# Products of zeros on TensorE between the steps of three mixture-of-experts routers

## The chip, the cores and the metric

The kernel runs on one core of a Trainium2 chip. The metric is the device time of one launch in microseconds (us), the median over several runs. TensorE's clock has two levels in what follows, 1.2 and 2.4 GHz, which the profile writes as a granted clock of 0.50 and 1.00.

## The reference

The reference runs one layer of a first block and two layers of a second block on 256 tokens of width 1024, all in float32. Each of the three layers ends in a hierarchical mixture of experts. Its router is what matters here:

```python
g_logits = jnp.dot(t, w_rg).astype(jnp.float32) + b_rg          # 4 groups
g_idx = jnp.argmax(g_logits, axis=-1)
e_logits = (jnp.dot(t, w_re) + b_re).reshape(n_tok, 4, 8)       # 32 experts
e_sel = e_logits[rows, g_idx]                                   # those of the chosen group
top_v, top_i = lax.top_k(e_sel, 2)
top_w = jax.nn.softmax(top_v, axis=-1) * g_w[:, None]
for g in range(N_GROUPS):
    h = silu(einsum('td,edf->tef', t, w_gate[g])) * einsum('td,edf->tef', t, w_up[g])
    out = out + einsum('tef,efd->td', h * combine[:, g, :, None], w_down[g])
```

Every token goes to two of 32 experts. The experts' hidden width is 256 in the first layer and 512 in the other two, so the expert weights are 100.7 MB and twice 201.3 MB, and they are most of what the kernel reads.

## The kernel before, in words

**Parts.** The program is a straight line for each engine, with semaphores between them. On TensorE it goes: mixers of layer 1, `moe("e1")`, mixers of layer 2, `moe("e2")`, mixers of layer 3, `moe("e3")`. The function `moe` of the TensorE block (lines 737 to 916) has a router, a loop over experts, and a branch for experts with too many tokens.

**Router, on TensorE.** `residual` (or, in e2 and e3, code in the main program) computes the last output projection (line 663, 1106 or 1150) and transposes the first 128 tokens (line 643). `moe` then

- multiplies the first 128 tokens by the router's weights (line 750, 8 matmuls of 36 columns);
- waits for VectorE to finish the second 128 tokens, first half (`_tok1a`) and second half (`_tok`), and transposes them in two groups of four (`turn_to_T`, line 643);
- waits until ScalarE (line 1197) and VectorE (line 1465) have copied those transposes out of PSUM, and multiplies them by the router's weights (line 750 again);
- writes zeros into PSUM banks 0 to 3 with one product each of the bfloat16 tile `no_sum`, which holds zeros (line 757); the scatter matmuls of the loop add to these banks later;
- waits for VectorE's choice of experts (`_sel`, lines 1646 to 1670) and counts the rank of each token within its expert by five small float32 matmuls (lines 761 to 765, "the rank matmuls") into bank 7;
- waits for VectorE to turn ranks into a selection matrix S (lines 1676 to 1697; `_split`), and gathers the tokens of the first step's experts by 32 matmuls (`gather`, line 774) into banks 4 and 7;
- waits until ScalarE and VectorE (line 1711) have copied those, and begins the loop with the first gate products (line 820).

**Loop over experts.** A step takes 4 experts in e1 and 2 in e2 and e3: gate and up products (line 820), the next step's gather (774), transposes (829, 834), down products (852), scatter (864). There are 8 steps in e1 and 16 in each of e2 and e3.

**Weights.** SyncE issues all loads of weights into `ring`, six slots of 2 MB, which hold the weights of exactly one step. The first step's weights are loaded before or during the router (lines 526 to 530); the load of a later step's weights into a slot waits until the matmuls that read the slot are done (lines 516 to 518, `used[hs]`). 

**PSUM banks.** A table made in Python (`plan`, `uses`) says which use of each bank is which; `bank_free[b]` counts the reads that free bank b, and TensorE waits for that count before it writes a bank again. Bank 7 is free from the last attention on until the rank matmuls; banks 0 to 3 hold zeros or sums of the scatter from line 757 on.

Of the kernel before, what the change touches and what calls it, by code (L numbers as in the profile page):

```python
# [28 lines left out]
P = 128  # L29
# [58 lines left out]
def build(nc, ins, out):  # L88
    ctx = ExitStack()
    with ctx:  # L90
        _build(ctx, nc, ins, out)


def _build(ctx, nc, ins, out):
    def sb(name, shape, dt=F32):
        return ctx.enter_context(nc.sbuf_tensor(name, shape, dt))
# [3 lines left out]
    def flag(name):  # L100

        if name not in sems:
            sems[name] = ctx.enter_context(nc.semaphore(name))
        return sems[name]
# [12 lines left out]
    no_sum = sb("no_sum", [P, 512], mybir.dt.bfloat16)  # L117
# [130 lines left out]
    psum = ctx.enter_context(nc.psum_tensor("psum", [P, 8, 512], F32))  # L248
# [4 lines left out]
    bank_free = [flag(f"bank_free{b}") for b in range(8)]  # L253
    plan, uses = {}, [0] * 8

    def use(name, bank):
        plan[name] = (bank, uses[bank])
        uses[bank] += 1
# [3 lines left out]
    def use2(*name):  # L262
        use(name, turn[0] % 2)
        turn[0] += 1
# [38 lines left out]
    for n in range(4):  # L303
        use2("res1", n)

    def plan_moe(name):
        for n in range(4):
            use((name + "xT", n), (4, 5, 2, 3)[n] if name == "e3" else 2 + n)
        use((name + "logits",), 6)
        use((name + "rank",), 7)  # L310

    plan_moe("e1")
    before_moe = {"e1": list(uses)}
    use(("memk",), 5)
# [11 lines left out]
    for n in range(4):  # L326
        use(("res2", n), 2 + n)
    plan_moe("e2")
    before_moe["e2"] = list(uses)
    plan_turn("x3T", 4)  # L330
# [11 lines left out]
    for n in range(4):  # L342
        use(("res3", n), (0, 1, 2, 3)[n])
    plan_moe("e3")
    before_moe["e3"] = list(uses)

    def open_bank(pe, *name):

        b, m = plan[name]
        if m:  # L350
            pe.wait_ge(bank_free[b], m)
        return b

    def close_bank(ins, *name):
        ins.then_inc(bank_full[plan[name][0]], 1)
# [10 lines left out]
    def evacuated(eng, *name):  # L366

        b, m = plan[name]
        eng.wait_ge(bank_free[b], m + 1)
# [19 lines left out]
    for part, (names, width) in enumerate(zip(STREAM, (3, NSLOT, NSLOT))):  # L389
# [5 lines left out]
        e = f"e{part + 1}"  # L395
# [7 lines left out]
    def load_chunk(sp, c):  # L403
        s, _, prior = where[c]
        if isinstance(prior, str):
            full(sp, *last_use[prior])
        else:
            for half in range(2):
                if prior[half]:
                    sp.wait_ge(used[2 * s + half], prior[half] + SEED)  # L410
        sp.dma_start(ring[:, s, :], ins["stream"][CHUNKS.index(c)]).then_inc(loaded[2 * s], 16)
# [42 lines left out]
    def after(eng, who, name):  # L454

        eng.wait_ge(finished[who], milestones[who].index(name) + 1)
# [13 lines left out]
    def moe_wait(eng, e, name, value):  # L470

        eng.wait_ge(flag("moe_" + name), value + (before_layer(e, name) + SEED))
# [18 lines left out]
    def _(sp):  # L491
# [14 lines left out]
        for part, e in enumerate(("e1", "e2", "e3")):  # L506
# [32 lines left out]
            with sp.If(n > 0):  # L539
                with sp.Fori(0, n) as k:  # L540
                    for w, (hs, per, _) in enumerate(moe_slots(e, 0)):
                        expert = sp.value_load(ovf[0:1, bass.ds(k * X + (NOVF + w % X), 1)], min_val=0, max_val=NE - 1)
                        sp.wait_ge(used[hs], moe_used[e][hs] + STEPS[e] // 2 * per + SEED)
                        sp.wait_ge(flag(e + "_ovf_pe"), k * OVF_PE + (2, 2, 4)[w // X])
                        sp.dma_start(moe_view(e, hs), ins[e + ("_gate", "_up", "_down")[w // X]][expert, :, :]).then_inc(
                            flag(e + f"_ovf_loaded{w // X}"), 16)
                sp.wait_ge(flag("moe_sum_ready"), int(e[1]))
# [77 lines left out]
    def _(pe):  # L625
        mm = pe.matmul
# [7 lines left out]
        def turn_to_T(name, src, ready=None, which=range(4)):  # L634


            for n in which:
                th, kk = n // 2, n % 2
                if ready and ready[n]:
                    after(pe, "vec", ready[n])  # L640
                b = open_bank(pe, name, n)
                for k in range(4):
                    last = pe.transpose(psum[:, b, k * P:(k + 1) * P], src[:, th, (4 * kk + k) * P:(4 * kk + k + 1) * P], ident[:, :])
                close_bank(last, name, n)
# [14 lines left out]
        def to_tok(w, c0, c1, name, th, lhs, k0=0, K=KD, start=True, stop=True, close=True):  # L659

            b = open_bank(pe, *name) if start else plan[name][0]
            for k in range(K):
                last = mm(psum[:, b, 0:c1 - c0], lhs[:, k0 + k, th * P:(th + 1) * P], w[:, k, c0:c1],  # L663
                          start=(start and k == 0), stop=(stop and k == K - 1))
            if close:
                close_bank(last, *name)
            return last
# [59 lines left out]
        def residual(name, chunks, lhs, e, tok):  # L727

            w = [chunk(pe, c, D) for c in chunks]
            for n in range(4):  # L730
# [3 lines left out]
                to_tok(w[0], hf * 512, hf * 512 + 512, (name, n), th, lhs, 0, 4, True, False, False)  # L734
                to_tok(w[1], hf * 512, hf * 512 + 512, (name, n), th, lhs, 4, 4, False, True, True)

        def moe(e, tok):
            F = 2 if e == "e1" else 4
            FW = F * P
# [3 lines left out]
            b = open_bank(pe, e + "logits")  # L743
            for th in range(TH):
                if th:
                    turn_to_T(e + "xT", tok, (None, None, e + "_tok1a", e + "_tok"), range(2, 4))
                evacuated(pe, e + "xT", 2 * th)
                evacuated(pe, e + "xT", 2 * th + 1)
                for k in range(KD):
                    last = mm(psum[:, b, th * NR:(th + 1) * NR], xT[:, k, th * P:(th + 1) * P], wr[:, k, :],  # L750
                              start=(k == 0), stop=(k == KD - 1))
# [3 lines left out]
            for b in range(4):  # L755
                pe.wait_ge(bank_free[b], before_moe[e][b])
                mm(psum[:, b, :], no_sum[:, 0:P], no_sum[:, :], start=True, stop=False, skip_group_check=True)

            b = open_bank(pe, e + "rank")
            after(pe, "vec", e + "_sel")  # L760
# [9 lines left out]
            def gather(par, half):  # L770
# [4 lines left out]
                                  S[:, par, th, :], start=(th == 0), stop=(th == TH - 1))  # L775
                last.then_inc(flag(("moe_gathA", "moe_gathB")[half]), 1)

            after(pe, "vec", e + "_split")
            moe_wait(pe, e, "S", 1)
            gather(0, 0)  # L780
# [2 lines left out]
            with pe.Fori(0, STEPS[e] // 2) as i:  # L783
                for u in range(2):
# [75 lines left out]
                    for half in range(2):  # L860
                        if half:
                            moe_wait(pe, e, "outB", c(1))
                        for th in range(TH):
                            last = mm(psum[:, 2 * th + half, :], SwT[:, th * P:(th + 1) * P], og[:, half * 512:(half + 1) * 512],  # L864
                                      start=False, stop=False, skip_group_check=True)
# [9 lines left out]
            with pe.If(n > 0):  # L875
                with pe.Fori(0, n) as k_:
# [10 lines left out]
                    for g in range(2):  # L887
                        pe.wait_ge(flag(e + f"_ovf_loaded{g}"), k_ * (16 * X) + 16 * X)
                        wv = [moe_view(e, moe_slots(e, 0)[X * g + x][0]).rearrange("p (k n) -> p k n", k=KD) for x in range(X)]
                        for k in range(KD):  # L890
                            for x in range(X):
                                last = mm(psum[x * CAP:(x + 1) * CAP, 5 + g, 0:FW], xg[:, 0, k, x * CAP:(x + 1) * CAP], wv[x][:, k, :],
                                          start=(k == 0), stop=(k == KD - 1))
# [15 lines left out]
                    for half in range(2):  # L909
                        for th in range(TH):  # L910
                            last = mm(psum[:, 2 * th + half, :], SwT[:, th * P:(th + 1) * P], og[:, half * 512:(half + 1) * 512],
                                      start=False, stop=False, skip_group_check=True)
# [57 lines left out]
        for th in range(TH):  # L970
            for k in range(KD):
                last = mm(psum[:, b, th * 8:(th + 1) * 8], xT[:, k, th * P:(th + 1) * P], wf[:, k, :],
                          start=(k == 0), stop=(k == KD - 1))
# [60 lines left out]
        pe.wait_ge(flag("mixed"), 4)  # L1034
        residual("res1", ("wo0", "wo1"), mixedT, "e1", xh)
        moe("e1", xh)

        wait_T("memT")
# [58 lines left out]
        for ks in (range(MT, KD), range(MT)):  # L1097
            for n in range(4):
# [4 lines left out]
                for k in ks:  # L1103
                    if ks[0] == 0 and n == 0:
                        pe.wait_ge(flag("conv_out"), k + 1)
                    last = mm(psum[:, b, :], yT[:, k, th * P:(th + 1) * P], w[k // 4][:, k % 4, hf * 512:(hf + 1) * 512],  # L1106
                              start=(k == MT), stop=(k == MT - 1))
                if ks[0] == 0:
                    close_bank(last, "res2", n)
        moe("e2", x_sb)  # L1110


# [62 lines left out]
        for n in range(2, 4):  # L1175
            if n == 3:
                first_tokens("e3", x_sb)
            for k in (6, 7, *range(MT)):
                last = project_out(n, k, k != 6)
            close_bank(last, "res3", n)  # L1180
        moe("e3", x_sb)


# [1000 lines left out]
```

## Time and profile before

| | |
|---|---|
| median of 3 runs | 1851.45 us (1851.08 to 1854.99) |
| the profiled execution, its own time | 1852.89 us |
| its span | 1851.1 us |
| TensorE busy with matmuls | 1668.3 us, 90% of the span |
| VectorE, ScalarE busy | 545.7 us, 258.1 us |
| mean granted clock of TensorE | 0.946 |
| read from memory | 568.21 MB, a mean of 308 GB/s |

The span is the time from the first to the last instruction of the profiled execution, and 1.8 us of its own time lie outside it. Times of single instructions are counted from the span's start. "PE" is TensorE multiplying, "PEld" TensorE loading its stationary operand, "DVE" VectorE, "ACT" ScalarE, "SPq" SyncE's queue. A float32 matmul stands in the trace as two passes, so eight matmuls are "x16".

### The profile page before, as it was taken

The numbers are of one execution on the slowest core, as the hardware profiler recorded it, in microseconds if no ns is written. First come the engines' busy times: TensorE is split into PE (matmuls) and PEld (weight loads), VectorE is DVE, ScalarE is ACT, GpSimd is POOL, SyncE is SP. The second block draws the span as 40 slices with busy tenths as digits, with TensorE's granted clock in tenths as the row PEclk, the third lists the DMA queues.
The fourth block names the chain that finished last, engine by engine and source line by source line (L and its number), as shares of the span: only waits on it lengthen the run. The fifth ranks groups of instructions, "written<-read, shape, count | busy, mean of one in ns | idle before, by whom it ended". The sixth has DMA issues, their size and how long they took to land.

```text
span 1851.1 us, 28802 instructions
## 1 busy us (share of the span) xinstructions
PE 1668.3 (90%) x11753; PEld 886.4 (48%) x11757; DVE 545.7 (29%) x1276; ACT 258.1 (14%) x546; POOL 36.8 (2%) x63
## 2 busy tenths in 40 slices
PE   6888997677689988999999999799879999999996
PEld 4467755434368744434434343585443434434342
DVE  5896223110016743111111111423432111111113
ACT  2102201000012420101001010123211101111010
POOL 7000000000000000000000000000000000000000
PEclk9799997888889988999999999899979999999998
DMA  6222346999994125999999999632149999999993
GB/s 230 91 92 92 125 182 275 421 422 422 422 400 143 64 115 237 424 429 428 428 429 429 427 429 428 266 137 91 39 197 426 427 429 428 429 429 428 429 428 153
DMA packets 49559, 570.03 MB, mean 308 GB/s; under 512 B 5728, under 2 KB 7136, under 8 KB 9184
## 3 DMA queue, kind: packets, MB, share of 16 engines
q1 hardware_dynamic: 47648, 563.22, 73.0%
q10 hardware_dynamic: 1856, 6.06, 1.0%
q8 instruction: 36, 0.59, 0.1%
q14 instruction: 19, 0.16, 0.0%
HBM read 568.21 MB, written 1.05 MB: 308 GB/s over the span
## 4 chain that ended last, share of the span: by engine, by line
PE 66%; DMA 19%; DVE 8%; issue 2%; POOL 1%; ACT 1%; SPq 1%; PEld 0%; DVEq 0%; PEldq 0%; ACTq 0%; POOLq 0%
PE psum L820 23%; DMA ring<-in_e_up 17%; PE psum L852 9%; PE psum L655 8%; PE psum L774 6%; PE psum L864 5%; PE psum L663 3%; PE psum L717 2%; PE psum L1106 1%; PE psum L1066 1%; PE psum L697 1%; DMA ring<-in_e_down 1%; PE psum L1150 1%; DVE arena L1917 1%; PE psum L684 1%
## 5 line engine op out<-in xcount | busy, mean ns | idle before, releaser
L820 PE MATMUL psum<-ring,arena 128*32 128x512 f32 (+2 forms) x5120 | 523.7, 567 | 60.4 <-DMA ring<-in_e_up 41.7
L820 PEld LDWEIGHTS psum<-ring,arena 128*32 128x32 f32 x5120 | 173.5, 114 | 406.8 <-issue 396.7
L852 PE MATMUL psum<-ring,arena 128*32 128x512 f32 (+1 forms) x2304 | 255.5, 594 | 2.2 <-DMA ring<-in_e_down 2.2
L1737 DVE TENSOR_TENSOR arena<-arena,psum 128x512 f32<-128x512 f32 (+1 forms) x40 | 25.4, 634 | 595.8 <-PE psum L820 595.8
L655 PE MATMUL psum<-xT,ring 128*128 128x256 f32 x640 | 146.2, 390 | 5.1 <-DVE xT L1467 2.1
L774 PEld LDWEIGHTS psum<-arena,x_sb 128*128 128x128 f32 x1088 | 131.7, 198 | 34.4 <-issue 34.4
L864 PE MATMUL psum<-arena 128*128 128x512 f32 x320 | 148.0, 605 | 0.0
L774 PE MATMUL psum<-arena,x_sb 128*128 128x128 f32 x1088 | 140.9, 285 | 7.4 <-DVE arena L1697 7.4
L852 PEld LDWEIGHTS psum<-ring,arena 128*32 128x32 f32 x2304 | 70.9, 110 | 157.4 <-issue 157.4
L655 PEld LDWEIGHTS psum<-xT,ring 128*128 128x128 f32 x640 | 125.0, 197 | 25.4 <-issue 7.8
L864 PEld LDWEIGHTS psum<-arena 128*128 128x128 f32 x320 | 57.5, 189 | 90.9 <-issue 90.9
L1744 DVE COPY arena<-psum 128x512 f32<-128x512 f32 x40 | 27.7, 692 | 225.6 <-PE psum L852 225.6
L1250 ACT ACTIVATE arena<-psum 128x512 f32<-128x512 f32 (+1 forms) x40 | 22.2, 554 | 484.2 <-PE psum L820 484.2
L1230 ACT ACTIVATE arena<-psum 128x512 f32<-128x512 f32 x43 | 25.7, 597 | 387.3 <-PE psum L774 387.3
L1711 DVE COPY arena<-psum 128x512 f32<-128x512 f32 x43 | 29.7, 692 | 148.8 <-PE psum L774 148.8
L663 PE MATMUL psum<-ring,xT 128*128 128x512 f32 (+1 forms) x160 | 65.6, 571 | 0.0
L655 PE MATMUL psum<-arena,ring 128*128 128x256 f32 x192 | 45.7, 403 | 7.6 <-issue 5.1
L1256 ACT ACTIVATE arena<-psum 128x512 f32<-128x512 f32 x40 | 23.9, 597 | 187.0 <-PE psum L852 187.0
L2035 DVE SCALAR_TENSOR_TENSOR arena<-arena,vec 128x256 f32<-128x256 f32 x120 | 48.4, 480 | 0.0
L663 PEld LDWEIGHTS psum<-ring,xT 128*128 128x128 f32 x160 | 31.4, 197 | 32.2 <-issue 31.0
L655 PEld LDWEIGHTS psum<-arena,ring 128*128 128x128 f32 x192 | 39.0, 204 | 14.5 <-issue 8.6
L774 PE MATMUL psum<-arena 128*128 128x128 f32 x288 | 38.4, 291 | 1.6 <-DVE arena L1691 1.6
(317 smaller groups left out, 1319.6 us busy)
## 6 DMA issues: line engine op xcount, KB each, us to landing
ring<-in_e_down SPq DMA_DIRECT2D x64, 2048.0 KB, 15.6
ring<-in_e_gate SPq DMA_DIRECT2D x64, 2048.0 KB, 14.5
ring<-in_e_up SPq DMA_DIRECT2D x64, 2048.0 KB, 17.2
ring<-in_stream SPq DMA_DIRECT2D x27, 2048.0 KB, 11.9
ring<-in_e_gate SPq DMA_DIRECT2D x32, 1024.0 KB, 18.9
ring<-in_e_up SPq DMA_DIRECT2D x32, 1024.0 KB, 18.7
ring<-in_e_down SPq DMA_DIRECT2D x32, 1024.0 KB, 20.6
rows<-in_rows ACTq DMA_DIRECT2D x9, 512.0 KB, 5.3
```

Of the source, the lines that this page charges most:

```text
L655: last = mm(psum[:, b, n * T:(n + 1) * T], w[:, k, c * P:(c + 1) * P], rhs[:, k, :], start=(k == 0), stop=(k == K - 1))
L663: last = mm(psum[:, b, 0:c1 - c0], lhs[:, k0 + k, th * P:(th + 1) * P], w[:, k, c0:c1], start=(start and k == 0), stop=(stop and k == K - 1))
L717: last = mm(psum[:, b, n * T:(n + 1) * T], w[:, k, c * P:(c + 1) * P], rhs[:, k, :], start=(k == 0), stop=(k == KD - 1))
L774: last = mm(psum[:, (4, 7)[half], k * P:(k + 1) * P], tok[:, th, (4 * half + k) * P:(4 * half + k + 1) * P], S[:, par, th, :], start=(th = ...
L820: last = mm(psum[r, 5 + g, 0:FW], xg[:, u, k, r], w, start=(k == 0), stop=(k == KD - 1))
L852: last = mm(psum[r, (4, 7)[half], :], hT[:, f, r], w, start=(f == 0), stop=(f == F - 1))
L864: last = mm(psum[:, 2 * th + half, :], SwT[:, th * P:(th + 1) * P], og[:, half * 512:(half + 1) * 512], start=False, stop=False, skip_grou ...
L1230: act(xg[:, par, 0:4, :], psum[:, 4, :].rearrange("p (k c) -> p k c", k=4), ACT.Copy).then_inc(flag("moe_xgA"), 1)
L1711: ve.tensor_copy(xg[:, par, 4:8, :], psum[:, 7, :].rearrange("p (k c) -> p k c", k=4)).then_inc(flag("moe_xgB"), 1)
L1737: tt(hh[:, 0:FW], sg[:, 0:FW], psum[:, 6, 0:FW], ALU.mult).then_inc(flag("moe_h"), 1)
L1744: ve.tensor_copy(og[:, 512:1024], psum[:, 7, :]).then_inc(flag("moe_outB"), 1)
L2035: stt(out=conv[:, n, :], in0=hpad[:, n, bass.ds(i * TAP_STEP + (d + 1), T)], scalar=dw[:, bass.ds(i * TAP_STEP + (d + 1 + n * TAPS), 1)], ...
```

## The change

TensorE gets further products of the tile of zeros, each 128 x 128 by 128 x 512 in bfloat16, at four places of each router. Those into bank 7 open the sum anew, so they overwrite; those into banks 0 and 1 add zero to what stands there. `before_rank` keeps how often bank 7 has been used before the router, so that the products into it wait until its last reader is done. Nothing else is changed: 34 products in e1, 43 in e2 and 43 in e3 are added, 120 in all.

```diff
+    before_rank = {}
+
     def plan_moe(name):
         for n in range(4):
             use((name + "xT", n), (4, 5, 2, 3)[n] if name == "e3" else 2 + n)
         use((name + "logits",), 6)
+        before_rank[name] = uses[7]
         use((name + "rank",), 7)
...
+        def idle_products(bank, count):
+
+            after(pe, "pool", "no_sum")
+            for _ in range(count):
+                mm(psum[:, bank, :], no_sum[:, 0:P], no_sum[:, :], start=(bank == 7), stop=False, skip_group_check=True)
+
         def moe(e, tok):
...
             for th in range(TH):
                 if th:
+                    pe.wait_ge(bank_free[7], before_rank[e])
+                    idle_products(7, 8)
                     turn_to_T(e + "xT", tok, (None, None, e + "_tok1a", e + "_tok"), range(2, 4))
+                    idle_products(7, 3)
                 evacuated(pe, e + "xT", 2 * th)
                 evacuated(pe, e + "xT", 2 * th + 1)
                 for k in range(KD):
...
             for b in range(4):
                 pe.wait_ge(bank_free[b], before_moe[e][b])
                 mm(psum[:, b, :], no_sum[:, 0:P], no_sum[:, :], start=True, stop=False, skip_group_check=True)
+            idle_products(0, 18)
 
             b = open_bank(pe, e + "rank")
             after(pe, "vec", e + "_sel")
...
+            idle_products(1, 5 if e == "e1" else 14)
             after(pe, "vec", e + "_split")
             moe_wait(pe, e, "S", 1)
             gather(0, 0)
```

## Rows read from the trace of the kernel before

**Rows 1.** The page: DMA's busy tenths in 40 slices of the span.
```profile
DMA  6222346999994125999999999632149999999993
```
**Rows 2.** The chain that ended last, in order of time (start, us, what).
```profile
303.61 7.08 PE psum L820 x125
312.08 18.85 DMA ring<-in_e_up
...
720.17 1.98 PE psum L774 x16
...
1024.52 13.97 PE psum L820 x127
1038.94 21.69 DMA ring<-in_e_up
```
**Rows 3.** Windows: start:end, us, each engine's busy us, granted clock, DMA share, GB/s.
```profile
296.00:308.00 12.00, 10.71 (x116) 9.38 (x120) 3.23 (x12) 2.26 (x3) 0.00 (x0) 0.78 0.01 1
310.00:322.00 12.00, 12.00 (x92) 6.59 (x83) 4.63 (x10) 1.47 (x3) 0.00 (x0) 1.00 1.01 424
```
**Rows 4.** SyncE's timeline: the first loads issued after routers e1 and e2.
```profile
307.42 2.12 SPq L523 DMA_DIRECT2D ring<-in_e_gate  x4
...
713.51 0.88 SPq L523 DMA_DIRECT2D ring<-in_e_gate  x2
```
**Rows 5.** Timeline of router e1 (start, us, engine, line, what, [idle before <-releaser]).
```profile
276.55 1.87 PE L750 MATMUL psum<-wr,xT 128*128 128x36 f32 x16
...
280.17 0.65 PE L643 MATMUL psum<-ident,arena 128*128 128x128 f32 x4 [1.75 <-DVEq L452]
...
281.08 1.11 PE L643 MATMUL psum<-ident,arena 128*128 128x128 f32 x4 [0.26 <-DVEq L452]
...
282.23 0.60 ACT L1197 ACTIVATE xT<-psum 128x512 f32<-128x512 f32 x1 [3.33 <-PE psum L643]
...
282.97 3.60 PE L750 MATMUL psum<-wr,xT 128*128 128x36 f32 x16 [0.78 <-ACT xT L1197]
...
286.79 1.49 PE L757 MATMUL psum<-no_sum 128*128 128x512 bf16 x3 [0.22 <-issue]
...
292.00 0.61 PE L761 MATMUL psum<-arena,before 128*128 128x32 f32 x2 [3.72 <-DVEq L452]
...
293.70 0.61 PE L765 MATMUL psum<-arena,ones 128*128 128x32 f32 x2
...
295.90 6.41 PE L774 MATMUL psum<-arena 128*128 128x128 f32 x32 [1.59 <-DVE arena L1691]
```
**Rows 6.** Line 757: duration ns min/median/max, first and last start us, forms.
```profile
L757 PE MATMUL psum<-no_sum x9: 634/634/634, 286.8 to 1350.8; 128*128 128x512 bf16 x9
```
**Rows 7.** As Rows 5, of routers e2 (two rows) and e3.
```profile
680.62 2.01 PE L643 MATMUL psum<-ident,x_sb 128*128 128x128 f32 x8 [2.98 <-DVEq L452]
...
698.45 6.52 PE L774 MATMUL psum<-arena,x_sb 128*128 128x128 f32 x32 [3.70 <-DVE arena L1697]
...
1361.11 6.29 PE L774 MATMUL psum<-arena,x_sb 128*128 128x128 f32 x32 [3.70 <-DVE arena L1697]
```
**Rows 8.** Windows cut where the granted clock changes (columns as in Rows 3).
```profile
278.40:280.80 2.40, 0.65 (x5) 0.42 (x4) 1.71 (x4) 0.20 (x1) 0.00 (x0) 1.00 0.90 369
281.00:301.20 20.20, 13.81 (x58) 12.13 (x60) 8.43 (x40) 3.78 (x6) 0.00 (x0) 0.50 0.64 264
...
680.40:704.00 23.60, 14.97 (x63) 13.11 (x65) 11.96 (x53) 4.04 (x6) 0.00 (x0) 0.50 0.44 179
...
1342.60:1366.20 23.60, 14.50 (x61) 12.64 (x63) 12.42 (x53) 3.57 (x6) 0.00 (x0) 0.50 0.44 180
```
**Rows 9.** PE's timeline before router e3, and two windows of that stretch.
```profile
1329.21 1.97 PE L643 MATMUL psum<-ident,x_sb 128*128 128x128 f32 x8 [2.52 <-DVEq L452]
...
1328.80:1332.10 3.30, 2.89 (x10) 2.38 (x11) 2.37 (x4) 0.60 (x1) 0.00 (x0) 0.50 0.01 2
1332.20:1336.00 3.80, 3.80 (x10) 1.65 (x9) 0.00 (x0) 0.00 (x0) 0.00 (x0) 1.00 0.00 0
```

## The prediction

> **What bounds the kernel now.** I read the page's DMA slices first, for what kind of stages there are: long stretches at 9 tenths (the three loops over experts) with gaps between them [rows 1]. Then the chain that ended last, for what limits each stretch. In loop e1 every step ends in a wait for weights (18.85 us in the first) [rows 2]. In loop e2 TensorE itself is the chain until 1024.5 us, and only from there do steps end in DMA; it had started a full step of weights ahead, and uses them up slightly faster than they come. So both loops are in the end bound by a stream of weights, and the question for a router is whether that stream starts earlier when the router ends earlier. It does. Between 296 and 308 us DMA moved 1 GB/s, while from 310 to 322 us it moved 424 [rows 3]: the ring is full with the first step's weights, and SyncE issues the next load only when the first gate products free their slots, at 307.42 and 713.51 us, and likewise in e3 [rows 4]. The routers therefore stand wholly on the path, with both TensorE and DMA behind them, and a microsecond taken from one is a microsecond of the kernel. The first step's weights are no limit either: in e1, the tightest, they had landed before 296 us [rows 3], and the loop began at 303.61 [rows 2].
>
> Inside a router TensorE and VectorE alternate. The timeline of e1 [rows 5] shows which TensorE steps are on the chain, and the windows [rows 8] show at which clock: the granted clock is 1.00 until 280.8, then 0.50 until 301.2, so transposes, router products, ranks and most of the gather run at 1.2 GHz. In e2 and e3 it is 0.50 for 23.6 us each. Before each fall TensorE had been mostly idle (0.65 of 2.40 us busy in e1) [rows 8]. In the first loop it is also low after waits for DMA, which costs nothing there.
>
> **The change part by part.** It removes and moves nothing. What it gives is a clock that stays at 2.4 GHz through the router; what it costs is the time of 120 products.
>
> *Price of a product.* At 2.4 GHz the trace has none. Three of the old ones (line 757) at 1.2 GHz overlap to 1.49 us, and each by itself lasts 0.634, so they start (1.49 - 0.634) / 2 = 0.43 us apart, which is the price of one in a series [rows 5, 6]. The upper bound is thus 0.43. The same 16 router passes take 3.60 us at 0.50 and 1.87 at 1.00 [rows 5], a ratio of 1.93; so 0.22 us is my value and also about the lower bound, since 512 columns have to pass at twice the rate at best.
>
> *The gaps, product by product (e1).* (1) 8 products between 278.42 (276.55 + 1.87) and the transposes at 280.17: 1.76 us into 1.75. The second four transposes wait for VectorE until 281.08 anyway, so cost 0. (2) 3 products after the transposes: 0.66 us, into the 0.78 us in which the copies are made (ScalarE's is 0.60): 0; up to 0.5 in all if they ran at 1.2 GHz. (3) 4 old and 18 new products: 22 x 0.22 = 4.8 us. From the end of the router products (282.97 + 3.60 = 286.57) to the rank matmuls (292.00) VectorE's chain takes 5.4 us [rows 5], whatever the clock: 0, with 0.6 us to spare. If that cover failed, at 0.43 us they would last 9.5 us. (4) 5 products, 1.1 us, in the idle 1.59 before e1's gather, 14 products, 3.1 us, in the idle 3.70 of e2 and e3 [rows 5, 7]: 0. Nothing is queued behind a product except TensorE's own next step, and the new waits on banks 0, 1 and 7 are for readers that are long done. VectorE's and ScalarE's steps keep their length, and become the whole of what is left between TensorE's.
>
> *What the clock gives, per router.* Second transposes: four take 1.11 us at 0.50 and 0.65 at 1.00: 0.46. Router products of the second half: 3.60 - 1.87 = 1.73. Rank matmuls: ten passes from 292.00 to 294.31, 2.31 us; ten passes at the full-clock price of a router pass (1.87 / 16 = 0.117) are 1.17: 1.14. Gather: 32 passes take 6.41, 6.52 and 6.29 us [rows 5, 7]; 16 take 1.98 in the loop at full clock [rows 2], so 32 take 3.96: 2.45, 2.56, 2.33. Sum: 5.8 in e1, 5.9 in e2, 5.7 in e3, together 17.3 us. The e2 and e3 transposes are the same case: 8 in 2.01 us, of which VectorE's readiness, not the clock, sets the start of the second four [rows 7].
>
> *Does the clock stay up?* The weak place is the same in all three: second-half transposes, 3 products, the thin router products of 36 columns. In e2 it begins with 2.98 us of idle [rows 7], of which 8 products fill 1.8. I must assume that transposes and zeros count as work. Before router e3 the trace has a stretch that bears on the first: at a clock of 0.50, 1.97 us of transposes and only 0.92 us of matmuls (2.89 busy less 1.97) ran from 1329.2, and at 1332.2 the clock was 1.00 [rows 9]; e1's gather, all matmuls, needed from 295.9 to 301.2 to raise it [rows 5, 8]. So transposes count here. The Trainium skill says otherwise: "TensorE: Matmul & The Clock Gate", Part 4, holds that a transpose does not count as the engine being busy in the way a matmul does. By that rule the clock would fall in this place, which is the first rival below.
>
> *Sum.* The profiled execution took 1852.89 us, so 1852.89 - 17.3 = 1835.6 by its own time; it stands 1.44 us above the median of 1851.45, from which I count: **1834.2 us**. The stages between the loops also have short low-clock stretches, and where they lie will shift with the earlier routers; the low stretch of the three gathers differs by 0.5 us (5.3 us in e1 from 295.9 to 301.2, 5.55 in e2 from 698.45 to 704.0, 5.1 in e3) [rows 5, 7, 8]. With several such places I allow 2 us either way. Late next, in each router, is VectorE's chain of small operations.
>
> **The rivals.**
> (A) *The clock falls again between the second transposes and the router products.* Then the router products take 3.6 us, and of the 22 products those before the clock returns take 0.43. The gathers took 5.1 to 5.55 us of continuous work to bring it back; 5.3 us are 12 products, the other 10 take 2.2, in all 7.5 us against 5.4: the ranks come 2.1 us late. Kept are transposes, ranks and gather (0.5 + 1.1 + 2.5), less 2.1: 2.0 us, or 3 if the clock comes back earlier. Three times 2.5 is 7.5: 1844 us; if one or two routers do so, 1837.5 to 1841. For it: the thin place in e2 and e3. Against: rows 9, and 11 products and 8 transposes in it.
> (B) *Zeros do not count as work, the clock falls as before, and the products run at 0.43: slower.* The 3 products then end 1.3 us after the transposes, 0.5 late; the 22 take 9.5 us where 5.4 are free: 4.1 late; the 5 take 2.15 where 1.59 are free: 0.6; the 14 take 6.0 where 3.70 are free: 2.3. That is 5.2 in e1 and 6.9 in each of e2 and e3, 19 us: 1870 us. It decides from the point at which a product costs over 5.4 / 22 = 0.25 us. For it: before, 4 products of zeros at 286 us raised nothing [rows 8]. Against: they were 1.7 us of work, followed by 3.7 idle, and real matmuls of that length raised nothing either (the 2.3 us of ranks).
> (C) *The gain is hidden, no change*: the loop would have to wait for its first weights or the weight stream start by itself. Rows 3 and 4 speak against it; it would need a late first load, or TensorE to run the products elsewhere than written. 1851 us.
>
> **How the numbers follow.** My forecast has a chance of 0.77, A 0.13, B 0.06, C 0.04. The forecast's own range is 1834.2 - 4 (2 us of shifted clock, and up to 2 of the spread of the runs, 1.4 us between the profiled one and the median) to + 4, so 1830 to 1838. The range reaches on to A's 1844 and leaves out B, C and the tails: 1830 to 1844. About 0.2% (3.7 us) is what a measurement of this kernel can tell from no change. Faster by more: forecast and A, 0.90. Within: 0.04. Slower: 0.06.
>
> **What would show it.** Right: in the changed profile no 0.50 window from the last output projection to the first gate products in any router; second router products (line 750) in 1.9 us, gather in 4.0; the products 0.21 to 0.22 us apart; the first gate products 5.8, 11.7 and 17.3 us earlier in e1, e2 and e3, and SyncE's loads with them; the steps of the loops as long as before. Step (3) is wrong if the rank matmuls start directly behind a product instead of behind VectorE; the carrying-over is wrong if the loops' ends are not earlier by as much as their beginnings. The forecast as a whole falls if TensorE's clock is 0.50 anywhere in the second halves of the routers.

## The result, and the profile of the changed kernel

The changed kernel takes 1831.49 us (median of 4 runs, 1828.82 to 1836.10) beside 1853.09 us for the kernel before in the same series: a ratio of 0.9886, 95% interval 0.9859 to 0.9913. A second series gave 0.9884 (0.9863 to 0.9905). That is 21.6 us less, where 17.3 us were forecast, and 1834.2 us lies 0.15% above what was measured. What was forecast for the routers came; over a quarter of the gain came from somewhere else.

In the page the clock's slices with the three routers (the 7th, the 15th and 16th, and the 30th) now read 9:
```profile
span 1827.1 us, 29048 instructions
PEclk9799999888899999999999999899999999999998
DMA  6222347999994137999999999632159999999993
```
Windows over the whole of the three routers (start:end, us, busy us of each engine, granted clock, DMA share, GB/s) say it outright; they answer to [rows 8]:
```profile
276.60:298.20 21.60, 18.48 (x121) 12.71 (x119) 12.02 (x47) 5.10 (x9) 0.00 (x0) 1.00 0.74 298
665.60:690.40 24.80, 20.39 (x130) 13.59 (x128) 17.12 (x62) 4.37 (x7) 0.00 (x0) 1.00 0.56 218
1320.60:1345.20 24.60, 20.28 (x130) 13.59 (x128) 17.02 (x62) 4.38 (x7) 0.00 (x0) 1.00 0.54 214
```
The granted clock is 1.00 from end to end, where before it was 0.50 for 20 to 24 us. The timeline of router e1 (start, us, engine, line, what, [idle before <-releaser]) answers to [rows 5]:
```profile
276.74 1.87 PE L762 MATMUL psum<-wr,xT 128*128 128x36 f32 x16
278.44 1.89 PE L744 MATMUL psum<-no_sum 128*128 128x512 bf16 x8
280.36 0.66 PE L646 MATMUL psum<-ident,arena 128*128 128x128 f32 x4
281.27 0.66 PE L646 MATMUL psum<-ident,arena 128*128 128x128 f32 x4 [0.25 <-DVEq L455]
281.77 0.81 PE L744 MATMUL psum<-no_sum 128*128 128x512 bf16 x3
282.71 1.95 PE L762 MATMUL psum<-wr,xT 128*128 128x36 f32 x16
284.49 1.03 PE L769 MATMUL psum<-no_sum 128*128 128x512 bf16 x4
285.35 4.05 PE L744 MATMUL psum<-no_sum 128*128 128x512 bf16 x18
290.07 0.38 PE L774 MATMUL psum<-arena,before 128*128 128x32 f32 x2 [0.67 <-DVEq L455]
290.95 0.39 PE L778 MATMUL psum<-arena,ones 128*128 128x32 f32 x2
292.31 1.24 PE L744 MATMUL psum<-no_sum 128*128 128x512 bf16 x5 [0.97 <-DVE arena L1692]
293.39 3.73 PE L787 MATMUL psum<-arena 128*128 128x128 f32 x32
298.41 1.93 PE L834 MATMUL psum<-ring,arena 128*32 128x256 f32 x32 [1.29 <-DVE arena L1725]
```
Line 744 is the new product. 18 of them and the 4 of line 769 run from 284.49 to 289.40 and leave 0.67 us before VectorE's choice is ready. The gap that the prediction did not have stands in the last but two row: the group of 5 begins not behind the ranks, at 291.3, but 0.97 us later, released by VectorE's line 1692.

From the first router product to the first gate product the routers took 27.06, 30.46 and 30.24 us before, and take 21.67, 24.78 and 24.81 now: 16.5 us less. The loops behind them are as long as they were (223.99, 464.76 and 464.98 us from the first gate product to the last scatter; now 223.95, 464.33 and 464.24), so what a router gives is passed on whole. But the two profiled spans differ by 24.0 us. Of the other 7.5, 4.8 lie between loop e1 and router e2, 1.7 between loop e2 and router e3, and 1.2 in the loops; 0.2 are lost ahead of the first router. The chain of waits shows the largest piece, at the end of loop e1. Before (start, us, what):
```profile
523.96 3.65 PE psum L864 x8
527.61 5.10 issue
532.71 9.20 PE psum L655 x32
```
and after:
```profile
518.73 3.65 PE psum L878 x8
522.38 0.57 issue
522.95 2.40 PE psum L658 x10
525.35 1.50 issue
526.85 5.02 PE psum L658 x22
```
After the last scatter of e1 TensorE stood still for 5.1 us, with nothing that the profile shows to wait for; now it is 0.6 and, inside the projection, 1.5. From that scatter to router e2 it is 143.35 us in place of 148.18. The change doesn't touch this stretch, except that 34 products stand ahead of it in TensorE's program.

### The profile page after: what moved, and what is told of

Read it like the earlier page. It is cut to its first block, busy times and chain, and to the rows that moved or that the text cites. A ratio compares the mean times of both kernels' runs of the same rounds, so it can differ in the third digit from the quotient of the medians.

```text
span 1827.1 us, 29048 instructions
## 1 busy us (share of the span) xinstructions
PE 1673.2 (92%) x11876; PEld 879.7 (48%) x11877; DVE 545.3 (30%) x1276; ACT 258.2 (14%) x546; POOL 37.0 (2%) x63
## 4 chain that ended last, share of the span: by engine, by line
PE 69%; DMA 17%; DVE 8%; issue 2%; POOL 1%; ACT 1%; SPq 1%; PEld 0%; PEldq 0%; DVEq 0%; ACTq 0%; POOLq 0%
PE psum L834 24%; DMA ring<-in_e_up 16%; PE psum L866 10%; PE psum L658 8%; PE psum L787 6%; PE psum L878 5%; PE psum L666 3%; PE psum L720 2%; PE psum L1120 2%; PE psum L1080 1%; PE psum L700 1%; PE psum L1164 1%; DVE arena L1931 1%; PE psum L687 1%; PE psum L710 1%
## 5 line engine op out<-in xcount | busy, mean ns | idle before, releaser
L787 PEld LDWEIGHTS psum<-arena,x_sb 128*128 128x128 f32 x1088 | 126.7, 192 | 27.1 <-issue 26.8
L787 PE MATMUL psum<-arena,x_sb 128*128 128x128 f32 x1088 | 135.5, 278 | 0.0
L658 PEld LDWEIGHTS psum<-arena,ring 128*128 128x128 f32 x192 | 37.4, 196 | 11.3 <-issue 6.0
L666 PE MATMUL psum<-ring,arena 128*128 128x512 f32 (+1 forms) x96 | 36.6, 542 | 2.8 <-DMA ring<-in_stream 2.8
## 6 DMA issues: line engine op xcount, KB each, us to landing
ring<-in_e_up SPq DMA_DIRECT2D x64, 2048.0 KB, 17.1
ring<-in_e_down SPq DMA_DIRECT2D x32, 1024.0 KB, 20.5
```

What stands on the lines that cost most here:

```text
L658: last = mm(psum[:, b, n * T:(n + 1) * T], w[:, k, c * P:(c + 1) * P], rhs[:, k, :], start=(k == 0), stop=(k == K - 1))
L787: last = mm(psum[:, (4, 7)[half], k * P:(k + 1) * P], tok[:, th, (4 * half + k) * P:(4 * half + k + 1) * P], S[:, par, th, :], start=(th = ...
```

## The experiments

In what follows "the routers" are the three times from the first router product to the first gate product, "the pause" is TensorE's idle time without a releaser after e1, "the way" is the time from the last scatter of a loop to the next router, and "the tail" the time from the last scatter of e3 to the end of the span.

**The kernel before, again.** No edit.

> The kernel before, unchanged, for a second profile. In the first one TensorE stood still for 5.1 us after the loop of e1, with no releaser in the trace (reason: issue), and for 0.6 + 1.5 us at that place in the changed kernel. Theory L (the place of the instructions in memory decides how long that pause is): the pause is 5.1 us again, within 0.3. Rival R (it is chance in every execution): it differs by more than 1 us from the first profile. The routers from the first router product to the first gate product should last 27.1, 30.5 and 30.2 us as before.

1851.31 us. The pause is 5.18 us, as first seen, so it is no chance of one execution. The routers are 25.53, 29.40 and 30.66 us, together 2.2 us shorter than in the first profile and than expected: the low clock of router e1 lasted 17.1 us here and 20.5 there. So the 87.8 us of the first profile are one draw; over four kernels with unchanged routers (this one, the first, and the two with padding below) the sums are 87.8, 85.6, 87.4 and 88.0 us, 87.2 in the mean.

**34 small products at the start.** The kernel before, and:

```diff
         after(pe, "pool", "ident")
+        after(pe, "pool", "no_sum")
+        for _ in range(34):
+            mm(psum[:, 7, 0:8], no_sum[:, 0:P], no_sum[:, 0:8], start=True, stop=False, skip_group_check=True)
         after(pe, "vec", "h_tok")
```

> The kernel before with 34 products of 8 columns at the very start, where TensorE waits for VectorE; they are there to move all later TensorE instructions by as many places as the 34 products of router e1 do in the changed kernel, and the routers are as before (27.1, 30.5, 30.2 us). Theory L: the pause after e1 shrinks from 5.1 to 2.1 us as in the changed kernel, and the kernel is 3 to 5 us faster than before, 1847 to 1850 us. Rival T (the pause shrank because the router ended earlier, so by timing and not by place): the pause stays at 5.1 us and the time at that of before within 1 us.

1847.02 us, ratio 0.9966 (0.9955 to 0.9978). The routers are unchanged (27.10, 29.72, 30.58), the padding ran from 5.58 to 6.63 us where TensorE waits until 12.46, and the chain at the end of e1 has taken the shape of the changed kernel's:
```profile
529.05 0.50 issue
529.55 2.40 PE psum L655 x10
531.95 1.62 issue
533.56 4.91 PE psum L655 x22
```
Theory L stands, and T falls: nothing ended earlier here. The place of its instructions alone makes the kernel before 6.3 us faster (0.34%; the interval is 4.1 to 8.3). 4.9 us of that lie on the way to router e2: 3.0 are the pause (5.1 less 2.1), and 1.9 come from the clock, which no longer falls in it, so that the projection behind it takes 7.3 us of work instead of 9.2.

Another 1.5 us lie in the tail, which is 15.87 us instead of 17.40. The chain has this behind the last scatter, in the kernel before and in this one:
```profile
1832.84 2.40 issue
...
1829.35 0.03 issue
```
The changed kernel does not have that part: its tail is 17.42 us. At the end of e1 34 products stand ahead in both kernels, but at the end of e3 34 here and 120 there. So this run repeats the changed kernel's shift only as far as router e2, and its 6.3 us can't be carried over whole.

**128 small products at the start.** The same with `range(128)`.

> The kernel before with 128 products of 8 columns at the start, in place of 34. TensorE's code is loaded in pieces of 16 KB (the instruction queue moved 0.59 MB in 36 packets). Theory L16: a product's two instructions are 128 bytes, so 128 products shift the code by just one piece, its borders fall on the same instructions of the end of e1 as in the kernel before, and the pause is 5.1 us again; the kernel takes as long as before, 1852 us. Rival: the pause depends on the place in some other way, and is 0.5 to 4 us; the kernel is up to 5 us faster.

1853.77 us, ratio 1.0005 (0.9995 to 1.0014), and the pause is back:
```profile
529.14 5.05 issue
534.18 9.46 PE psum L655 x32
```
A shift by 128 products changes nothing, so what counts is the place within a stretch of that length. The page of the kernel before shows 0.59 MB in 36 packets, so 16 KB each, in the instruction queue q8, and this run has one packet more, which fits a product of two instructions of 64 bytes each. The third row is the kernel before again, from 527.61 to 532.71 us, the pause:
```profile
q8 instruction: 36, 0.59, 0.1%
q8 instruction: 37, 0.61, 0.1%
...
q8 instruction: 1, 0.02, 1.4%
```
The Trainium skill, "Runtime: NRT & Kernel Launch", section "Instruction fetch mechanics", says that code comes in blocks of 16 KB (256 instructions) and that a taken branch whose target is not there must wait for a fetch. The runs agree with the block's size, and the end of e1 is such a place: TensorE jumps over the branch for overflowing experts.

The traces also hold the time of each packet. In the kernel before one begins at 529.57 us, 2.0 us into the pause, and takes 1.17; TensorE goes on 2.0 us after its end. In each of the eleven profiles with a pause of over 1 us at this place, a packet of q8 overlaps the pause, and TensorE goes on 1.3 to 2.0 us after the packet's end. In the other two (runs late_only and best, below) it begins 1.6 and 1.8 us after TensorE has gone on, and nothing waits. So TensorE stands still there while its code is loaded. What the 1.3 to 2.0 us are is not shown, and whether the pause would be shorter if DMA did not move 429 GB/s of weights in it wasn't tried.

**11 more in the changed kernel.** The changed kernel with `range(11)` at the start.

> The changed kernel with 11 products of 8 columns at the very start, where TensorE waits anyway. Theory L (the place of TensorE's instructions decides the pause after e1): all instructions lie 45 products further than before instead of 34; with 0, 11, 23 and 34 of them the first pause was 5.1, 4.0, 0.5 and 0.5 us, and a second one of 1.5 us within the projection came at 34. So the first pause stays at 0.5 and the second moves to an earlier place in the projection or in front of it, within 0.5 us of its length. Routers as in the changed kernel. Rival T (timing, not place): pauses as in the changed kernel, in the same places.

1838.98 us, ratio 0.9922 (0.9906 to 0.9939), 6.6 us slower than the changed kernel in the same series. I had the details wrong: the second pause did not move within the projection, but all of it came back in front (4.77 us), and the way to e2 is 148.97 us. The conclusion stands all the same: eleven harmless products take away about as much as thirty-four had given. Up to 1.7 us of it is another matter: router e3 took 26.47 us in this profile, with 3.4 us of low clock behind its ranks, of which more below.

**Only the later products.** From the changed kernel:

```diff
-                    idle_products(7, 8)
...
-                    idle_products(7, 3)
```

> Only the 18 products after the router products and the 5 or 14 after the ranks are kept; the 8 and 3 in the thin first part are left out. Theory K (the clock must be held through the thin part, or it is lost for a while): the clock falls before the second transposes as in the kernel before, the second router products take 3.6 us, the 22 products need up to 7.5 us at first and bring the clock back before or during the ranks; ranks 2 us later than in the changed kernel, gather at the full clock. Per router a gain of 2 to 3 us over the kernel before, 1844 us in all. Rival Z (the early products are superfluous): the clock stays at 1.00 and the routers last 21.7, 24.8 and 24.8 us as in the changed kernel.

1839.35 us, ratio 0.9930 (0.9910 to 0.9951). The routers are 25.14, 28.65 and 27.61 us. The chain of e1 shows theory K at work:
```profile
284.78 3.60 PE psum L760 x16
288.38 1.71 PE psum L767 x4
290.08 5.31 PE psum L744 x18
295.40 0.14 PE psum L772 x2
```
The router products are slow (3.60), the first products of zeros run 0.43 us apart, and the ranks begin directly behind the last of them, so that TensorE and not VectorE releases them, 7.0 us behind the router products instead of 5.4. But during them the clock comes back, at 292.84 us, and ranks and gather run at the full one:
```profile
284.80:292.80 8.00, 8.00 (x27) 5.03 (x28) 3.61 (x18) 1.35 (x2) 0.00 (x0) 0.50 1.01 425
292.90:302.20 9.30, 8.33 (x59) 6.35 (x57) 3.89 (x19) 1.92 (x3) 0.00 (x0) 1.00 0.29 115
```
Zeros count as work: rival B of the prediction is out. The routers give 1.9 us each where 2 to 3 were expected, and the kernel is still 4.7 us faster than the 1844 of theory K, for a reason that has to do with the place, given below.

**Only the earlier products.** From the changed kernel:

```diff
-            idle_products(0, 18)
...
-            idle_products(1, 5 if e == "e1" else 14)
```

> Only the 8 and 3 products of the thin first part are kept; the 18 and the 5 or 14 are left out. Theory K: the clock holds through the second router products (1.9 instead of 3.6 us, transposes 0.65 instead of 1.1), then falls in the 4 us in which TensorE waits for VectorE's choice, so ranks take 2.3 us and the gather 6.3 to 6.5. Gain per router 2.2 us, in all 6.6: the routers last 24.9, 28.3 and 28.0 us. Rival Z (the clock once held would not fall): the routers last 21.7, 24.8, 24.8.

1840.49 us, ratio 0.9940 (0.9918 to 0.9962). The routers are 24.32, 27.92 and 28.11 us, within 0.6 us of what theory K expects. The sums of the routers are 81.4 us (later only), 80.4 (earlier only) and 71.3 (both), against 87.2: 5.8 and 6.8 us alone, 15.9 together. The parts seem to be worth more together than apart, since the earlier ones make the later ones cheap and the later ones keep what the earlier ones held; but the surplus of 3.3 us is little more than the 2.4 us by which the sums of unchanged routers differ. Both kernels are 4 to 7 us faster in all than their routers explain. The pause differs too (0.5 us with 23 more products ahead of it, 4.0 with 11), the ways to router e2 are 141.5 and 146.7 us instead of 148.2, and both tails are 1.5 us shorter (15.88 and 15.87).

**The changed kernel, again.** No edit.

> The changed kernel once more, beside the next ones. Routers 21.7, 24.8 and 24.8 us, pause after e1 0.6 us and 1.5 us within the first projection, ratio to before 0.989.

1832.38 us, ratio 0.9884 (0.9863 to 0.9905). The pauses are 0.50 and 1.98 us (0.6 and 1.5 expected), but router e2 took 26.18 us. In its timeline the 14 products, begun 0.97 us late, took 4.58 us where they need 3.2, and a window puts the cause there:
```profile
685.85 4.58 PE L744 MATMUL psum<-no_sum 128*128 128x512 bf16 x14 [0.97 <-DVE arena L1692]
685.20:688.60 3.40, 2.75 (x7) 1.02 (x8) 2.98 (x16) 0.00 (x0) 0.00 (x0) 0.52 0.12 39
```
So the weak place is not only where the prediction put it. The idle time before the ranks, the thin ranks and the late start of the last products make a second one, and the clock fell there in one router of six in two profiles of this kernel (and in one of three in the padded one).

**The last products directly behind the ranks.** From the changed kernel:

```diff
             close_bank(last, e + "rank")
+            idle_products(1, 5 if e == "e1" else 14)
             for b in range(4, 8):
                 pe.wait_ge(bank_free[b], before_moe[e][b])
...
-            idle_products(1, 5 if e == "e1" else 14)
             after(pe, "vec", e + "_split")
```

> The changed kernel with the last group of products (5 or 14) put directly behind the ranks, ahead of TensorE's waits for banks 4 to 7. Theory M (in the changed kernel these products start 1.2 us after the ranks because the wait for bank 7 is the wait for VectorE's reading of the ranks, and so end 0.3 to 0.5 us after the selection matrix is ready): the products start within 0.1 us of the ranks' end, the gather starts 0.5 us earlier in e1 and 0.3 to 0.4 us earlier in e2 and e3, routers 21.2, 24.4 and 24.4 us, 1.2 us in all, near what can be told. Rival V (the gather waits for VectorE's matrix anyway): the routers stay as long as they are.

1830.27 us, ratio 0.9875 (0.9859 to 0.9892); by the time alone this isn't told from the changed kernel. The profile tells it:
```profile
292.44 0.39 PE L778 MATMUL psum<-arena,ones 128*128 128x32 f32 x2
292.67 1.24 PE L744 MATMUL psum<-no_sum 128*128 128x512 bf16 x5
294.42 3.81 PE L788 MATMUL psum<-arena 128*128 128x128 f32 x32 [0.51 <-DVE arena L1705]
```
The 5 products follow the ranks at once, and the gather is now released by VectorE's selection matrix (line 1705). The routers are 21.28, 24.56 and 24.56 us, 0.9 us less in all, near theory M's 1.2.

**Without the 3 products in the thin part.** From run moved, `idle_products(7, 3)` is left out.

> Run moved without the 3 products between the second transposes and the second router products (8 ahead, 18 and 5 or 14 behind are kept). Theory K3 (the thin part needs them): in at least one of the three routers the granted clock falls before or during the second router products, which then take 3.6 us instead of 1.9, and that router lasts 1 to 3 us longer. Rival: the 8 ahead and the products behind suffice, the clock holds in all three, and the routers last 21.3, 24.6 and 24.6 us as in run moved.

1832.54 us, ratio 0.9894 (0.9879 to 0.9909). The routers are 22.07, 27.02 and 25.37 us, and the clock fell in all three: in e1 behind the router products, in e2 and e3 in the midst of them:
```profile
674.55 2.79 PE L761 MATMUL psum<-wr,xT 128*128 128x36 f32 x16 [0.78 <-ACT xT L1210]
677.14 1.90 PE L768 MATMUL psum<-no_sum 128*128 128x512 bf16 x4
678.83 5.75 PE L744 MATMUL psum<-no_sum 128*128 128x512 bf16 x17
```
Three products of 0.22 us, which hide behind a copy and cost nothing, are worth 4.1 us over the three routers, in one profile of each kernel. Theory K3 holds. The time is only 2.3 us above that of run moved; the tail, 15.88 us instead of 17.70, gives 1.8 us back. In e2 and e3 this is rival A of the prediction.

**The same for the layer norm before layer 3.** From run moved; TensorE waits there for VectorE's layer norm, and its clock was low for 17.1 us.

```diff
-        turn_to_T("x3T", x_sb, ("x3_0", None, "x3", None))
+        for _ in range(44):
+            mm(psum[:, 7, :], no_sum[:, 0:P], no_sum[:, :], start=True, stop=False, skip_group_check=True)
+        turn_to_T("x3T", x_sb, ("x3_0", None), range(2))
+        for _ in range(7):
+            mm(psum[:, 7, :], no_sum[:, 0:P], no_sum[:, :], start=True, stop=False, skip_group_check=True)
+        turn_to_T("x3T", x_sb, (None, None, "x3", None), range(2, 4))
```

> The kernel of run moved, and 44 products between the end of the loop of e2 and the first transposes of the third layer, and 7 between these and the second transposes. Before, TensorE waits there 9.9 us for the layer norm, its clock is 0.50 for 17.1 us, and the transposes take 1.97 us twice and the first projections 9.4 to 9.8 us for 32 passes. Theory: the clock stays at 1.00, the second transposes take 1.0, the first projections about 7; the way from the end of e2 to router e3 shortens by 3 to 3.5 us, and 1828 us against the changed kernel's 1831.5. Rival: VectorE and ScalarE bound this place, and the gain is under 1 us.

1826.96 us, ratio 0.9857 (0.9841 to 0.9874). The clock stays up, the projection takes 7.14 us instead of the 9.67 of run moved, and the way to router e3 is 163.40 us instead of 165.7. It is 2.3 us and not 3 to 3.5, because a pause of the kind seen after e1 came between the products, so that they ended late:
```profile
1157.74 2.53 PE L1128 MATMUL psum<-no_sum 128*128 128x512 bf16 x11 [0.36 <-PE psum L878]
1161.73 7.08 PE L1128 MATMUL psum<-no_sum 128*128 128x512 bf16 x32 [1.46 <-issue]
1168.65 1.04 PE L646 MATMUL psum<-ident,x_sb 128*128 128x128 f32 x8
```
The transposes follow the last product directly: 11.3 us after the scatter, not the 9.9 after which the layer norm is ready. That 1826.96 us is still under the 1828 expected is no proof of this gain: against run moved the tail is 1.8 us shorter and the way to router e2 2.2 us longer. The way to router e3 is what the edit gives.

**All together.** Run gap3 with `range(37)` in place of 44, and `range(117)` small products at the start.

> Run gap3 with 37 products instead of 44 in the long wait at the end of e2 (there a pause of 1.5 us came between the products, so that they ended 1.4 us after the layer norm was ready), and 117 products of 8 columns at the start. With the 34 of router e1 that makes 151 = 128 + 23, and at 23 (run late_only) the pause after e1 was 0.5 us and the projection behind it had none. Theory L16: so it is here, and the transposes of the third layer are not held up: 2 + 1.4 us less than gap3, 1823.5 us. Rival (the place works otherwise): a pause of 2 to 5 us after e1, 1825 to 1829 us.

1825.08 us, ratio 0.9847 (0.9834 to 0.9861), 27.9 us less than the kernel before in this series; against the changed kernel's 0.9886 and 0.9884 it is 7 us faster, of which about 1.6 are the tail (15.87 us) and so the place. The place at the end of e1 was chosen by the rule of 128 and came out as forecast:
```profile
522.78 0.50 issue
523.28 7.14 PE psum L658 x32
```
and the transposes of layer 3 wait for VectorE again:
```profile
1155.38 7.93 PE L1131 MATMUL psum<-no_sum 128*128 128x512 bf16 x36 [0.36 <-PE psum L878]
1164.96 1.09 PE L646 MATMUL psum<-ident,x_sb 128*128 128x128 f32 x8 [1.64 <-DVEq L455]
```
The routers are 21.29, 24.57 and 24.57 us and the ways 143.29 and 162.58. The time is 1.6 us above the forecast of 1823.5, and by itself it would fit the rival's 1825 to 1829 as well; it is the pause of 0.50 us that decides between the two.

## Why the prediction was right, and where it was off

**That a router's microsecond is a microsecond of the kernel: right.** The argument was that SyncE's loads wait for the first gate products. The loops lasted as long as before to within 0.8 us.

**The price of a product: right.** 0.22 us was taken; the four of line 769 start 0.86 us ahead of the 18 of line 744, so one takes 0.215.

**That transposes and zeros count as work, and the clock stays up: right for the place that was named.** It held in the thin part in all routers that had the 8 and the 3. By how little is seen from run without3. The Trainium skill ("TensorE: Matmul & The Clock Gate", Part 4) says that a transpose does not count as the engine being busy in the way a matmul does; by that rule the clock would have fallen there, as the prediction's rival A has it, and it didn't. These routers don't test the rule by itself, since 11 products of zeros stand around the 8 transposes; that transposes alone would hold the clock wasn't tried.

**What the clock gives, per router: right in kind, 1 to 2 us too much over the three.** Second router products 1.95 us for 3.60 (forecast 1.87), second transposes 0.66 for 1.11, ranks 1.27 for 2.31, gather 3.73 to 3.8 for 6.3 to 6.5. The term that was mis-sized is in step (4), "5 products, 1.1 us, in the idle 1.59 ... : 0", with the sentence that the waits on the banks are for readers that are long done. The prediction looked at the waits that the change adds and not at those behind which the new products come to stand: `idle_products(1, ...)` is behind the old loop of waits on banks 4 to 7, and bank 7's is for VectorE to read the ranks. The products started 0.97 us late, and the gather began behind them; run moved gets 0.9 us back. Against the single profile from which I worked, the routers gained 5.39, 5.68 and 5.43 us instead of 5.8, 5.9 and 5.7. That is 16.5 us in all; against the mean of four unchanged sets (87.2) it is 15.9, and over both profiles of the changed kernel (71.3 and 72.6) it is 15.2.

The prediction also said that the forecast as a whole falls if the clock is 0.50 anywhere in the second half of a router. In the first profile it was not; in the second it was, for 3.4 us of router e2. With the last products directly behind the ranks it stayed up in all nine routers of runs moved, gap3 and best.

**"It removes and moves nothing": wrong, and this is the step that failed.** The change moves every later TensorE instruction. Three profiles have TensorE's code in its old place within a block (the kernel before twice, and pad128) and two are of the changed kernel; the means of their spans differ by 21.6 us. 15.2 of these are in the routers, 4.2 on the way to router e2, 1.4 on the way to router e3 and 0.8 elsewhere. The 4.2 come from the place: run pad34, with the same number of products ahead and no help to any router, has 4.9 there. The 1.4 are of the size by which unchanged kernels differ there (165.3 to 167.8 us), and stay open. The profile before had the sign of it, 5.1 us of "issue" on the chain in front of a projection that needed nothing; the prediction didn't ask what that pause was. Its own list of signs shows the gap: the first gate products should come 5.8, 11.7 and 17.3 us earlier, and they came 5.2, 15.7 and 23.3 earlier.

That the forecast lies only 2.7 us from the result is in part luck. It counted 2.1 us too much for the routers and left out 6.4 that came elsewhere, and it started from a median of 1851.45 us where the series has 1853.09. Without the 6.4 us the kernel would take about 1837.9, still in the range; with 45 products ahead of the end of e1 instead of 34 it took 1838.98, a gain of 14.5 us.

**The rivals.** A (the clock falls between the second transposes and the router products) didn't happen. A fall behind the ranks did, in one router in six, and cost 1.4 us; and with 3 products fewer the clock fell in all three routers. B (zeros don't count) and C (the gain is hidden) are out.

## What to carry to other kernels

Where an engine with a clock that follows its work waits for others on the critical path, work on nothing in exactly those waits pays if it ends before the wait does and leaves no thin stretch; look for the stretch with the least work, since one fall undoes the group of products behind it too. Check at which waits the filler itself comes to stand in the program, as it must begin when the real work ends. And when a change adds or removes instructions in a long program with branches, run the old kernel with the same number of harmless instructions beside it, before the difference is explained.

## What the runs showed of the hardware that I had not expected

The place of TensorE's code decides a pause of 0.5 to 5.2 us behind one jump. By the number of added products ahead of it, the pauses in front of and within the projection were 5.1 and 0 (0 and 128 added), 4.0 and 0 (11), 0.5 and 0 (23, and again 151), 0.5 and 1.4 (31), 0.5 and 1.5 to 2.3 (34), 4.8 and 0 (45). In each pause of over 1 us a 16 KB packet of TensorE's instruction queue was under way. The end of e3 is a second such place: the tail is 17.4 to 18.0 us with 0, 120, 128 or 131 added products ahead of it, and 15.9 with 33, 34, 87, 111, 171 or 281.

In router e1 of run late_only TensorE ran 3.6 us of router products without a gap and the clock stayed low; it rose 4.7 us after the first product of zeros behind them, so after 8.1 us of unbroken work, where the gather of the kernel before had run for 5.4 us when it rose [rows 5, 8]. How long a low clock lasts differs between executions of one kernel too: router e1, unchanged, took 27.1 us in one (20.5 of them at the low clock) and 25.5 in another (17.1).
